# Attention's end in another order, and GpSimd in VectorE's place for the memory attention's weights, in a four-layer encoder

## The reference

```
for layer in range(4):
    p = x @ w_in[layer]                                  # one input projection
    mixed = mixer(p)                                     # attention: softmax(qk) of two maps, w = p0 - lam*p1, w @ v, rms norm per head
    q, (km, vm) = p[..., -256:], split(mem @ w_kv[layer])
    probs = softmax(q @ km.T / 8)                        # memory attention, 4 heads
    recalled = probs @ vm
    x = layer_norm(alpha * x + concat(mixed, recalled) @ w_o[layer])
    x = layer_norm(alpha * x + conv_ffn(x))
```

## Time and profile before

| | |
|---|---|
| median of 3 runs | 1243.83 us (1242.46 to 1243.92) |
| the profiled execution, its time | 1243.12 us |
| its span | 1241.0 us |
| mean granted clock of TensorE | 0.998 |
| TensorE busy | 1228.3 us, 99% |
| VectorE busy | 1037.2 us, 84% |
| ScalarE busy | 720.6 us, 58% |
| GpSimd busy | 26.8 us, 2% |

### The profile page before, as it was taken

One profiled execution on the slowest core, in us unless ns is written; L12 is line 12 of the kernel. 1 busy time (PEld: TensorE's weight loads), 2 busy tenths in 40 slices (PEclk: granted clock), 3 DMA queues, 4 the chain that ended last, 5 costly groups with the idle time before them and its releaser, 6 DMA issues.

```text
span 1241.0 us, 19585 instructions
## 1 busy us (share of the span) xinstructions
PE 1228.3 (99%) x7290; PEld 1076.8 (87%) x7290; DVE 1037.2 (84%) x1613; ACT 720.6 (58%) x1170; POOL 26.8 (2%) x37
## 2 busy tenths in 40 slices
PE   9999999999999999999999999999999999999997
PEld 8988888888999998888889888888888988888886
DVE  6896888889779888988888978988888786988887
ACT  6674765555776546655554546655554674755552
POOL 0011000000000100000000000000000011000000
PEclk9999999999999999999999999999999999999999
DMA  9874575555553344656654774666555673666651
GB/s 339 278 235 160 189 249 190 187 187 169 170 184 123 119 148 166 227 191 201 189 187 170 246 255 167 223 200 194 192 187 174 210 238 113 225 205 199 198 190 53
DMA packets 79993, 239.75 MB, mean 193 GB/s; under 512 B 8694, under 2 KB 24694, under 8 KB 78876
## 3 DMA queue, kind: packets, MB, share of 16 engines
q1 hardware_dynamic: 79900, 238.51, 58.2%
HBM read 232.18 MB, written 6.30 MB: 192 GB/s over the span
## 4 chain that ended last, share of the span: by engine, by line
PE 92%; DVE 3%; ACT 2%; DMA 1%; issue 1%; SPq 1%; DVEq 0%; ACTq 0%
PE pair L844 29%; PE acc L938 21%; PE pair L847 14%; PE pair L876 4%; PE pair L877 3%; PE pair L878 3%; PE acc L844 2%; PE pair L1109 2%; PE acc L919 2%; PE acc L918 2%; PE acc L917 2%; DMA raw<-in_stream 1%; PE acc L847 1%; ACT ex L1304 1%; PE pair L1063 1%
## 5 line engine op out<-in xcount | busy, mean ns | idle before, releaser
L1365 DVE TENSOR_TENSOR w_lo<-raw,w_hi 128x1024 fp32r<-128x1024 f32 x400 | 482.5, 1221 | 89.7 <-ACT w_hi L1127 88.3
L1127 ACT ACTIVATE w_hi<-raw 128x1024 fp32r<-128x1024 f32 x400 | 419.9, 1057 | 220.1 <-PE pair L847 71.2
L844 PE MATMUL pair<-xT,w_hi 128*128 128x512 f32 x1520 | 478.0, 396 | 0.2 <-DVE w_lo L1365 0.2
L847 PEld LDWEIGHTS pair<-xT,w_lo 128*128 128x128 f32 x1520 | 285.6, 188 | 67.2
L847 PE MATMUL pair<-xT,w_lo 128*128 128x256 f32 x1520 | 298.9, 278 | 0.0
L844 PEld LDWEIGHTS pair<-xT,w_hi 128*128 128x128 f32 x1520 | 233.7, 189 | 3.5 <-DVE w_lo L1365 0.4
L1174 ACT ACTIVATE hid<-pair 128x512 f32<-128x512 f32 x88 | 52.6, 598 | 125.6 <-PE pair L847 125.6
L1406 DVE TENSOR_TENSOR hid<-pair,hid 128x512 f32<-128x512 f32 x88 | 60.6, 689 | 48.1 <-ACT hid L1174 47.7
L876 PE MATMUL pair<-xT,w_hi 128*128 128x256 f32 x336 | 97.4, 290 | 0.0
L877 PE MATMUL pair<-xT,w_hi 128*128 128x256 f32 x336 | 95.0, 283 | 0.0
L878 PE MATMUL pair<-xT,w_lo 128*128 128x256 f32 x336 | 95.0, 283 | 0.0
(11 more groups left out here) (229 smaller groups left out, 1654.3 us busy)
## 6 DMA issues: line engine op xcount, KB each, us to landing
raw<-in_stream SPq DMA_DIRECT2D x400, 512.0 KB, 4.7
gains<-in_ln SPq DMA_DIRECT2D x8, 1024.0 KB, 8.8
swap_scratch<-ex SPq DMA_DIRECT2D x24, 128.0 KB, 2.6
bias<-bias_scratch SPq DMA_DIRECT2D x2, 1152.0 KB, 8.3
raw<-in_stream SPq DMA_DIRECT2D x8, 256.0 KB, 6.0
swap_scratch<-prob SPq DMA_DIRECT2D x32, 64.0 KB, 4.3
a_sq<-swap_scratch SPq DMA_DIRECT2D x8, 256.0 KB, 2.9
xprobT<-swap_scratch SPq DMA_DIRECT2D x3, 512.0 KB, 3.9
```

The source lines that it names most:

```text
L844: pe.matmul(bank, w_hi[:, slot, kk * P:(kk + 1) * P], xT[:, kk].rearrange("p a s -> p (a s)"), start=(kk == 0), stop=(kk == KT - 1), skip_ ...
L847: last = pe.matmul(bank[:, 0:SEQ], w_lo[:, slot, kk * P:(kk + 1) * P], xT[:, kk, 0, :], start=False, stop=(kk == KT - 1), skip_group_check ...
L1127: nc.scalar.activation(w_hi[:, u % SPLIT, :], raw[:, u % RAW, :], ACT.Copy).then_inc(hi_ready, 1)
L1365: v.tensor_tensor(w_lo[:, u % SPLIT, :], raw[:, u % RAW, :], w_hi[:, u % SPLIT, :].bitcast(F32), ALU.subtract).then_inc(lo_ready, 1)
```

## The change

Three things. (1) The items at attention's end are put in another order: `pv 2` and `pv 3` come ahead of `turnw 4`, `turnw 5` comes behind the second half of the first WO chunk, `pv 4` and `pv 5` come half a WO chunk later, behind `scale 1`, and `scale 2` comes a half chunk later, into the held chunk. (2) With `late_unit`, the rounding and splitting of unit 2c+5 of the last V chunk stand behind that chunk's second half and its items (`scale 0`, `prob 5`, `spread 3`). (3) `xprob` is cut in two: VectorE keeps the reciprocal and signals `inv_ready`; GpSimd multiplies, in four instructions of 256 columns, and signals `xprob_ready`; VectorE waits for that ahead of `xswap`, which together with `xfetch` stands half a chunk later in the attention and convolution layers. In the convolution layer the second `xprob` stands half a chunk earlier.

```diff
+    def chunk(form, role, layer, index, between=(), after=(), held=False, late_unit=False):
...
-        if not held and c > 1:
+        if not held and not late_unit and c > 1:
             split_units(2 * c + 1 + AHEAD)
         items.append(("half", c, 1))
...
         items.extend(after)
+        if late_unit:
+            split_units(2 * c + 1 + AHEAD)
...
-                  2: [it("xexp", 1), it("xprob", 0), it("xswap", 0), it("xfetch", 0)],
-                  3: [it("xprob", 1), it("xswap", 1), it("xfetch", 1)],
-                  5: [it("log", 0), it("log", 1)], 6: [it("exp", 0)], 7: [it("exp", 1)],
+                  2: [it("xexp", 1), it("xprob", 0)], 3: [it("xswap", 0), it("xfetch", 0), it("xprob", 1)],
+                  4: [it("xswap", 1), it("xfetch", 1)], 5: [it("log", 0), it("log", 1)], 6: [it("exp", 0)], 7: [it("exp", 1)],
...
-                  16: [it("spread", 2)],
-                  17: [it("scale", 0), it("prob", 5), it("spread", 3)],
-                  18: [it("turnw", 4), it("pv", 2), it("pv", 3), it("turnw", 5)],
-                  19: [it("pv", 4), it("pv", 5), it("ms", 1), it("tok", 1), it("ms", 2)], 20: [it("scale", 1), it("tok", 2)],
-                  21: [it("scale", 2)]}
+                  16: [it("spread", 2)], 17: [it("scale", 0), it("prob", 5), it("spread", 3)],
+                  18: [it("pv", 2), it("pv", 3), it("turnw", 4), it("ms", 1)], 19: [it("turnw", 5), it("tok", 1)],
+                  20: [it("scale", 1), it("pv", 4), it("pv", 5), it("ms", 2), it("tok", 2)], 22: [it("scale", 2)]}
...
-            at = {0: [it("xlog", 0), it("xexp", 0), it("xlog", 1), it("xexp", 1), it("xprob", 0), it("xswap", 0), it("xfetch", 0)],
-                  6: [it("xprob", 1), it("xswap", 1), it("xfetch", 1)], 13: [it("xpv", 0), it("xpv", 1)]}
+            at = {0: [it("xlog", 0), it("xexp", 0), it("xlog", 1), it("xexp", 1), it("xprob", 0)],
+                  1: [it("xswap", 0), it("xfetch", 0)], 5: [it("xprob", 1)], 6: [it("xswap", 1), it("xfetch", 1)], 13: [it("xpv", 0), it("xpv", 1)]}
...
-                  held=role == "WO" and index[0] == 2)
+                  held=role == "WO" and index[0] == 2, late_unit=(role, index) == ("V", 2))
...
-                    link(v.reciprocal(row_inv[:, s, :], row_sum[:, s, :]))
+                    inverse = v.reciprocal(row_inv[:, s, :], row_sum[:, s, :])
                     if name == "xprob":
-                        last = v.tensor_tensor(prob[:, s].rearrange("p i t s -> p (i t) s"),
-                                               ex[:, s].rearrange("p i t s -> p (i t) s"),
-                                               row_inv[:, s, :].rearrange("p (j one) -> p j one", one=1).broadcast_to([P, 4, SEQ]),
-                                               ALU.mult)
...
+                        inverse.then_inc(inv_ready, 1)
                     else:
+                        link(inverse)
...
                 elif name in ("xswap", "swap"):
                     n = weights_of(item)
+                    if name == "xswap":
+                        dve.wait_ge(xprob_ready, xprob_ord[n])
...
+                elif name == "xprob":
+                    n = prob_ord["x", item[1], item[2]]
+                    s = n % 2
+                    pool.wait_ge(inv_ready, xprob_ord[n])
+                    for i in range(2):
+                        for t in range(TT):
+                            last = nc.gpsimd.tensor_scalar(prob[:, s, i, t, :], ex[:, s, i, t, :], row_inv[:, s, 2 * i + t:2 * i + t + 1],
+                                                           None, ALU.mult)
+                    last.then_inc(xprob_ready, 1)
```

More of the change, by code:

```diff
@@ L81, in make_schedule @@
     LATER = {"UA": "taps", "UB": "taps"}
-    def chunk(form, role, layer, index, between=(), after=(), held=False):
+    def chunk(form, role, layer, index, between=(), after=(), held=False, late_unit=False):
         c = len(chunks)
@@ L277, in trunk_kernel @@
     prob_ord = {(items[pos][0][:-4],) + items[pos][1:]: n for n, pos in enumerate(prob_pos)}
+    xprob_ord = {n: k + 1 for k, n in enumerate(n for n, pos in enumerate(prob_pos) if items[pos][0] == "xprob")}
     swap_count, swap_ord, turned_ord, seen = {}, {}, {}, {}
@@ L503, in trunk_kernel @@
         logits_done, max_ready, exp_ready = sem("logits_done"), sem("max_ready"), sem("exp_ready")
+        inv_ready = sem("inv_ready")
         xprob_ready, xprob_turned, xprobT_ready, swapped = sem("xprob_ready"), sem("xprob_turned"), sem("xprobT_ready"), sem("swapped")
@@ L607, in ex_free @@
                 return swap_stored[n % 2], 64 * swap_count[n]
-            return xprob_ready, items[prob_pos[n]][2] + 1
+            return xprob_ready, xprob_ord[n]
         def swap_source(n):
@@ L1012, in _ @@
                     n = prob_ord["x", item[1], item[2]]
-                    pe.wait_ge(xprob_ready, ordinal[pos] + 1)
+                    pe.wait_ge(xprob_ready, xprob_ord[prob_ord["x", item[1], item[2]]])
                     for i in range(2):
```

## The result

The changed kernel took 1252.03 us (median of 4 runs, 1250.95 to 1253.24) beside 1243.22 us for the kernel before on the same chip: ratio 1.0065, 95% interval 1.0052 to 1.0078. It is slower, by 8.8 us; 1241.1 with a range from 1238.0 to 1245.0 was forecast. The profiled execution took 1251.96 us for a span of 1249.8, 8.8 more than before. Ratios leave out executions at a much lower granted clock; there was one, of experiment 11 (1338.76 us at 0.85).

The account below looks back on a forecast made before the run. TensorE, busy 99% of the span, was taken as the bound, so only its waits or lower clock could be won. Layer 0 -3.0 + 0.4, layer 2 +0.9, layer 3 -1.0: -2.7 us, 1241.1 against the 1243.83 median; range 1238.0 to 1245.0.

Parts of the forecast that it names:

- Part 1: Attention's end reordered in layers 0 and 3: each end takes 17.2 us, gaining 3.0 and 1.0 us.
- T0: End of WO's first half chunk, from which each attention end is measured: 91.97 in layer 0, 1020.32 in layer 3, before.
- the closing wait: Attention's end, layers 0 and 3: the closing chunk waits 1.0 us for scale 2's residue, behind two splits queued on VectorE.
- The -4.0 given to both layers: Gain of the reordered end: 3.0 us in layer 0 and 1.0 us in layer 3.
- its 1.2 us: Attention's end: with one unit's rounding and splitting moved behind, ScalarE and VectorE reach L1679 some 1.2 us sooner.
- I take 0.40 each: Assumed price in us of each of 32 GpSimd products of 128x256: half the copy's columns plus something for a second operand.
- 7p - 2.4: Layer 0's delay in us, with p the price of one GpSimd product; 0.4 late at p = 0.4.
- 0.9 + 4 x 0.53: Layer 2's TensorE wait at CB1, forecast as 0.9 + 4(p - 0.4), p being a GpSimd product's price; 0.9 at 0.4.
- The rival "slower": Product price p = 1.0, the power's: +4.6, +3.3, +2.5 against -4.0, so +6.4, 1250; decides from p = 0.75; chance 0.10.
- The clock was missed: Clock loss was treated in layer 0 only; rival of it falling there anyway: 1.6 back, 1242.7, chance 0.07.
- "The swaps' stores and fetches ... nothing": SyncE's queue: stores and fetches go out up to half a chunk later, at no cost.
- That neither engine runs beside the other: GpSimd's products and VectorE's splits exclude each other; side by side, the sum would be 1.5 us better, -4.2.

Follow-up runs that it names:

- experiment 11: Kernel before with only the new order of attention's end, the unit split at its old place: 1241.29 us, ratio 0.9983.
- experiment 12: Reordered end and late split, product on VectorE at old places, plus the split ahead of the held WO chunk's first half moved behind it: 1240.1 us, ratio 0.9975.
- experiment 1: Changed kernel with the product back on VectorE at its old places, leaving the reordered end and late split: 1240.47 us, ratio 0.9983 to the kernel before.
- experiment 2: Kernel before with only GpSimd's product and its new places, attention's end in its old order: 1253.95 us, ratio 1.0091.
- Experiment 3: Changed kernel with the product back on VectorE but at the new places: 1245.66 us, ratio 1.0025 to the kernel before.
- experiment 5: Changed kernel with one GpSimd multiplication of 1024 columns in place of four of 256: 1245.79 us, ratio 1.0023 to the kernel before.
- experiment 6: Changed kernel with layer 2's product back on VectorE at its old places: 1247.74 us, ratio 1.0041 to the kernel before.
- experiment 7: Changed kernel with the transposes later by another half chunk or more: 1258.63 us, ratio 1.0122 to the kernel before.
- experiment 8: Reordered end, product on VectorE, new places of product, transpose and fetch in the attention layers alone: 1244.13 us, ratio 1.0006 to the kernel before.
- experiment 9: Reordered end, product on VectorE, new places in layer 2 alone: 1243.03 us, ratio 0.9997 to the kernel before.
- experiment 4: Kernel before with six idle GpSimd instructions of each of eight kinds added in layer 3's ConvFFN: 1249.0 us (one run).

## Why the prediction was wrong, point by point

- **Part 1 was right in mechanism.** From T0 to the closing chunk 17.35 and 17.33 us were measured against 17.2; the closing wait is 0.8 against 1.0 and hangs for the most part on the queued splits (experiment 12). L1030's wait and the lower clock of layer 0 are gone. The -4.0 given to both layers was -3.7 in the traces of the changed kernel (2.85 and 0.85) and of experiment 1, but about -2 in the runs of experiment 1 and, by the difference of experiment 2, -3. Part of the gap is argued, not shown: some 1.6 of the 3.0 in layer 0 is clock that the profiled execution before had lost, and 12 of the 21 executions of the kernel before beside experiment 1 had a mean granted clock of 0.999, as kernels without such a stretch have, against the 0.998 of the profiled one. What I did not see is that moving one split would have won as much by itself: I counted its 1.2 us and gave the gain to the order.
- **The failed step is "I take 0.40 each".** The product takes 0.93, and its length costs some 5 us (0.0040 to 0.0042: the changed kernel against experiments 3 and 5). I scaled a copy by columns and added a little for an operand; a copy was the wrong kind of instruction to scale, and the row of the power, 1.01, was nearer. Put into the working's own formulas, p = 0.93 gives 7p - 2.4 = 4.1 in layer 0 (3.4 measured), 0.9 + 4 x 0.53 = 3.0 in layer 2 (2.94 measured, at the chunk and line named), and some 2.2 in layer 3, by the rival's 2.5 at p = 1.0 (2.7 measured). The rival "slower" had the right places and its sum at this price is about +5.3. That the two attention layers come out so near is in part luck: with the product at half the length (experiment 5) the same steps give 1.0 and nothing, and TensorE still waited 1.8 and 1.6 there. The wait for the store that frees `ex` may be part of that; the rest stays open. Layer 2's formula held both times (3.0 and 1.2 against 2.94 and 1.0). The chance of 0.10 was too low: no row excluded it, and its point of decision (0.75) was below the one arithmetic row that the trace had.
- **The clock was missed.** The forecast counted it only in layer 0. Waits of 2.9 and 1.9 us in layers 2 and 3 each had a stretch at the 1.2 GHz level behind them, 3.3 us together. That is most of what lies between +5.3 and the 8.8 of the span. Not each such wait does it: experiment 6 waits 2.1 at the same place of layer 3 with no low window behind, as the kernel before did after 1.6; and the changed kernel's own wait of 1.9 in layer 0 had none.
- **"The swaps' stores and fetches ... nothing" was wrong as well.** Experiment 3 prices the places at 5 us without GpSimd. In the attention layers part of it is shown: the exponentials wait for the store that frees `ex` (experiments 7 and 8). The three kernels with a shorter product in the new places have this wait (1.2, 2.1 and 2.2 us in experiments 3, 5 and 8). In the changed kernel itself, and in experiments 2 and 6, which keep its product in these layers, it doesn't appear, presumably since VectorE's lateness at the reductions covers it. Experiment 3's profiled execution was the fastest of its ten runs (1242.86), so its trace shows less than its median costs; where the other 3 us of its median went stays open, as does the split of experiment 9's cost.
- **That neither engine runs beside the other** was right for VectorE's instructions with both inputs in SBUF, and stronger than I used it; L1413, with one input in PSUM, runs beside GpSimd (experiment 4). The changed kernel's longest product, 1.977 us, is one of 0.92 and nearly a split of 1.2; experiment 4 shows VectorE held for whole GpSimd instructions. The Trainium skill says so too (GPSIMD Engine Reference, section 1: VectorE instructions with two inputs in SBUF contend with GpSimd). Section 4.1 of that page of the Trainium skill calls GpSimd with one input "roughly line-rate"; here the trace disagrees: 0.92 us for 256 columns by a factor per row. From section 3.1 of that page of the Trainium skill my estimates were 0.56 for a product with two tensor inputs, 0.79 at the shortest here, and 0.22 for one input, 0.92 here.

## What to carry to other kernels

A price for an instruction that the trace does not have should come from an instruction of the same kind, and where there is none the engine's dearest row deserves as much of the chance as its cheapest (here it was the nearer one): measure it in an idle stretch first. Work given to an idle engine is not free when another engine must stand in its queue for the result, and a step moved later must be followed to the buffer it frees, not only to the data it delivers. When an end stands still, try moving the one instruction queued ahead of the late one before reordering the end.

## What the hardware showed that was not expected

- GpSimd's product by a factor per row: 0.44, 0.61, 0.92 and 1.64 us for 64, 128, 256 and 512 columns; with a constant factor 0.85 for 256, a copy 0.40, a product of two tensors 0.79, one of 1024 columns with broadcast factors 1.95 (shortest of six each).
- GpSimd work that nobody waits for slowed the kernel by 6.6 us (one run): it held VectorE's instructions with two inputs in SBUF (4.14 us for two that take 0.87) until TensorE waited 4.4 us, and the clock fell behind that. One with an input in PSUM kept its 0.68 us.
- TensorE's waits of 2.94 and 1.94 us in the changed kernel had a stretch at the 1.2 GHz level behind them that cost 1.7 and 1.6 us (windows at 0.50 to 0.72); waits of 1.93 (changed kernel), 2.0 (experiment 2) and 2.1 us (experiment 6) had none.
